# Who subtracts the weights' low parts in the mixer: from GpSimd to VectorE

## The chip, the cores and the metric

One core of a Trainium2 chip runs the whole program. The metric is the device time of one execution in microseconds (us). The kernel before took 1982.04 us, the median of three runs (1978.26 to 1982.62).

## The reference, cut to what matters

Two layers of a hybrid transformer work on 528 tokens (16 meta tokens and 512 others) of width 1024, in float32:

```python
for l in range(DEPTH):                       # DEPTH = 2
    h = mixer_block(h, ...)                  # w_in, three attentions, gates, w_branch, w_o
    h = conv_ffn(h, ...)                     # w_up, conv of width 3, silu(gate) * val, w_down
```

`mixer_block` norms `h`, multiplies it by `w_in` (queries, keys and values of three kinds of attention, and three sets of gates), norms the heads' queries and keys, runs the attentions (8 heads each), multiplies each branch by its `w_branch` and its sigmoid gate, sums them, and multiplies by `w_o`. `conv_ffn` is an up product of 2 x 2816 columns, a causal convolution of width 3, a gated silu, and a down product.

## The kernel before, in words

Activations lie with the width on the 128 partitions and the 528 tokens along the free dimension. All weights are packed on the host into **blocks** of 128x128 in the order in which TensorE takes them, and eight blocks make a **chunk** of 128x1024 float32 (512 KB). A layer has 1080 blocks, 135 chunks: 488 blocks (61 chunks) belong to the mixer's projections, gates and branch products, the rest to `w_o`, the up and the down product. There are 270 chunks in all, numbered c = 0 to 269.

Each product keeps float32 accuracy with three products in the fp32r format: high(x) by high(W), low(x) by high(W), high(x) by low(W) (lines 1357, 1360 and 1362, each as two halves of 264 tokens). So each chunk must be split into a high part `wh`, a copy of `raw` that is rounded to fp32r, and a low part `wl` = `raw` - `wh`. The pipeline for chunk c is:

- SyncE loads it into one of two `raw` buffers (`load`, line 734), once the low part of chunk c - 2 is done, since that was the last reader of the buffer.
- VectorE casts `raw` to `wh` (`high_part`, line 1670). It waits for the load, and for TensorE to have started chunk c - 2, so that one of the three `wh` and `wl` buffers is free.
- GpSimd subtracts (`chunk_low`, line 817) in four pieces of 128x256, since a long instruction of it would hold other work up. Chunk 0 alone has its low part from VectorE (line 1750).
- TensorE waits for the low part at the chunk's first block.

Both splitters work two chunks ahead (`AHEAD = 2`): the place of chunk c in the program of VectorE and of GpSimd is where block 8(c - 2) stands.

The order of everything else in the mixer is one plan (`mixer_plan`): for each event (a norm's statistics, a mask, a row maximum, a reciprocal, a head's copy) it has the block at which it stands, and each engine's program is the sorted list of its own events with the blocks between them. TensorE runs the blocks with the attention's small products in between. VectorE runs the row maxima (line 1962 and, for the meta tokens, 1940), the masks (line 1985), the norms' Newton steps (lines 1686, 1688 and 1691) and the products behind them (1887, 1902, 1906, 1909), the reciprocals of the softmax sums (1993), the scaling of projections (1822, 1830, 1832), and the gated sums (1839, 1844). ScalarE takes exponentials and the high parts of queries, keys and heads. GpSimd subtracts the low parts of these (lines 943, 954, 983, 992, 1001), fills constants into the attention's operands (831, 881 to 886) and copies the decay rows (918). Engines are in order: what stands behind a waiting or a long instruction is late. In the feed-forward part the casts and subtractions stand between the convolution's steps.

Of the kernel before, what the change touches and what calls it, by code (L numbers as in the profile page):

```python
# [9 lines left out]
P = 128  # L10
# [89 lines left out]


LATE = {'sk': 2, 'cq': 2, 'fv': 1}


def constants():
# [69 lines left out]
class Tile:  # L175


    def __init__(self, kind, m, i):
        self.kind, self.m, self.i = kind, m, i
        self.nk = BLOCKS[kind]  # L180
        self.slot = i % 2
        self.freed = None
        self.joint = None
        self.n = None
        self.raw = None


def mixer_plan():
# [105 lines left out]
    for j, (br, p) in enumerate(JOBS):  # L294
        b = BEGIN[j]
        if br == MLA:
            if p < 2:
                put(b - M_LEAD - 9, 4, "ones", j)
        elif j > 0:
            put(b - M_LEAD - 9, 4, "extras", j)  # L300
            put(b - M_LEAD - 5, 4, "extras2", j)
        if br == SWA:
            put(b - M_LEAD - 4, 7, "kfill", j, 0)
            put(b - M_LEAD - 3, 7, "kfill", j, 1)
        parts = [(e, q) for e in range(2) for q in (("4", "3", "2", "1") if br == SWA else ("4a", "4b", "3", "2", "1"))]
# [12 lines left out]
        put(b + PV_LAG, 4, *place(("PVM", j)))  # L318
        i = b + ST_HEAD + 4 + PV_LAG + 2
        for q in range(4):  # L320
            put(i + q, 6, "recip", j, q)
# [4 lines left out]
    blocks = [(i, 9, 0, ("block",) + order[i]) for i in range(len(order))]  # L326

    plan = {"tiles": tiles, "order": order}
    for engine in ("pe", "dve", "act", "pool", "sp"):
        mine = [(i + LAG.get((engine, step[0]), 0), rank, n, step) for i, rank, n, step in events]  # L330
        mine = sorted(blocks + mine, key=lambda x: x[0:3])
        plan[engine] = [x[3] for x in mine]

# [49 lines left out]
    return b  # L383


PLAN = weight_plan(mixer_plan()["order"])
CHUNKS = DEPTH * len(PLAN) // BLK
assert len(PLAN) % BLK == 0


def build(nc, W, H, PRM, CST, POS, OUT, SCR, counts):
# [50 lines left out]
    skh = sb("skh", [P, T], F32R, offset=gsb_at)  # L442
    skl = sb("skl", [P, T], F32R, offset=gsb_at + T * 4)
    mixer_end = at[0]

    at[0] = act_at
    ah = sb("ah", [P, FT, T], F32R)
# [69 lines left out]
    s_hi = nc.alloc_semaphore("chunk_high_part")  # L517
    s_lo = nc.alloc_semaphore("chunk_split")
    s_start = nc.alloc_semaphore("chunk_started")
    ready_made = S("small_tiles_ready")  # L520
    tile_ready = S("tile_ready")
    residual_updated = S("residual_updated")
# [56 lines left out]
    meta_done = S("meta_product_done")  # L579
    meta_heads_copied = S("meta_heads_copied")  # L580
    heads_copied = S("heads_copied")
    heads_ready = S("heads_ready")
    heads_high = S("heads_high_part")
    heads_low = S("heads_low_part")
# [22 lines left out]
    def frees(t):  # L607
        if t.kind == "ff":
            return rope_copied, ()
        if t.kind in NORMED:  # L610
            if t.kind == "cq" and t.m == 0:
                return copied, (t.i,)
            return (stat_copied if t.kind == "mq" else stat_taken), (t.i,)
        if t.kind in ("fv", "sv"):
            return values_scaled, (t.kind, t.m)
        if t.kind == "mv":
            return values_copied, (t.kind, t.m)
        if t.kind == "g":
            return gate_taken, t.m
        return gate_used, t.m  # L620

    previous = {}
    for a, b in zip(tiles, tiles[2:]):
# [100 lines left out]
    with block as blk:  # L724

        @blk.sync
        def _(sp):

            def load(n):
                if n >= CHUNKS:  # L730
                    return
                if n >= RAW:
                    sp.wait_ge(s_lo, n - RAW + 1)
                sp.dma_start(raw[:, n % RAW, :], W[n, :, :]).then_inc(s_raw[n % RAW], 16)

            def advance(l, i):
# [15 lines left out]
            for l in range(DEPTH):  # L752
                n_blocks = 0
                for s in plan["sp"]:
                    if s[0] == "block":
                        advance(l, n_blocks)
                        n_blocks += 1
                    elif s[0] == "extras":
                        j = s[1]
                        br, p = JOBS[j]  # L760
# [39 lines left out]
        def _(pool):  # L800
# [6 lines left out]
                    sem, n = began["last"]  # L807
                    pool.wait_ge(sem, n)

            def chunk_low(c):  # L810
                if c >= CHUNKS:
                    return
                pool.wait_ge(s_hi, c + 1)
                settled()
                for a in range(0, CW, CW // 4):
                    part = slice(a, a + CW // 4)
                    ins = nc.gpsimd.tensor_tensor(wl[c % SPLIT][:, part], raw[:, c % RAW, part],  # L817
                                                  wh[c % SPLIT][:, part].bitcast(F32), ALU.subtract)
                ins.then_inc(s_lo, 1)
                began["last"] = (s_lo, c + 1)  # L820

            def advance(l, i):
                n = l * LB + i
                if n % BLK == 0:
                    chunk_low(n // BLK + AHEAD)

            def fill(t, lo, hi, i, e, c0, c1, value, by=1):

# [21 lines left out]
            settled()  # L850
            pool.sem_inc(zeroed.sem, zeroed.tick((0, 0)))
            for c in range(1, AHEAD):
                chunk_low(c)
            for l in range(DEPTH):
                n_blocks = 0
                for s in plan["pool"]:
# [151 lines left out]
        def _(act):  # L1008
# [29 lines left out]
            act.dma_start(prm[:, :, :], PRM[:, :, :]).then_inc(s_prm, 16)  # L1038
            logarithms()

            def high_input(l, k):

                nc.scalar.activation(xh[:, k, :], h[:, k, :], ACT.Identity,
                                     scale=prm[:, l, PC_N1 + k:PC_N1 + k + 1]).then_inc(
                    high_ready.sem, high_ready.tick((l, "n1", k)))

            act.wait_ge(s_prm, 16)
            for k in range(KD):
                if k % 2 == 0:
# [2 lines left out]
                nc.scalar.activation(merged[:, k, :], h[:, k, :], ACT.Square).then_inc(  # L1052
                    residual_squared.sem, residual_squared.tick((-1, "dn", k)))
            for l in range(DEPTH):
                for s in plan["act"]:
                    if s[0] == "layer stat":
                        if s[1] != (l == 0):
                            continue
                        logarithms()
# [239 lines left out]
                def square_residual(which, k):  # L1299
                    act.wait_ge(residual_updated.sem, residual_updated.at(l, which, k))  # L1300
                    if k >= 2:
                        act.wait_ge(sum_ready.sem, sum_ready.at(l, which, k - 2))
                    nc.scalar.activation(hsq[:, k % 2, :], h[:, k, :], ACT.Square).then_inc(
                        residual_squared.sem, residual_squared.tick((l, which, k)))

                for k in range(KD):
                    act.wait_ge(residual_updated.sem, residual_updated.at(l, "wo", k))
                    nc.scalar.activation(xh[:, k, :], h[:, k, :], ACT.Identity,
                                         scale=gain[:, l, PC_N2 + k:PC_N2 + k + 1]).then_inc(
# [8 lines left out]
                for f in range(FT):  # L1318
                    for side, dst in ((0, cg), (1, cv)):
                        t = 2 * f + side  # L1320
                        m = side * FT + f
                        act.wait_ge(up_scaled.sem, up_scaled.at(l, t))
                        cw = PC_CW + 3 * m
                        nc.scalar.activation(dst[:, f % 2, skip:T], full(SLOTS[t % 4])[:, skip:T], ACT.Identity,  # L1324
# [7 lines left out]
                    copy(ah[:, f, skip:T], cv[:, f % 2, skip:T]).then_inc(act_high.sem, act_high.tick((l, f)))  # L1332
                if l + 1 < DEPTH:
                    act.wait_ge(tile_ready.sem, tile_ready.at(l, "up", 2 * FT - 1))
                    for k in range(KD):
# [6 lines left out]
        def _(pe):  # L1342

            def weights(n):

                c = n // BLK
                if n % BLK == 0:
                    pe.wait_ge(s_lo, c + 1)
                a = n % BLK * P
                return wh[c % SPLIT][:, a:a + P], wl[c % SPLIT][:, a:a + P]  # L1350

# [310 lines left out]
        def _(dve):  # L1662

            def high_part(c):
                if c >= CHUNKS:
                    return
                dve.wait_ge(s_raw[c % RAW], 16 * (c // RAW + 1))
                if c >= SPLIT:
                    dve.wait_ge(s_start, c - SPLIT + 2)
                nc.vector.tensor_copy(wh[c % SPLIT][:, :], raw[:, c % RAW, :]).then_inc(s_hi, 1)  # L1670

            def advance(l, i):
                n = l * LB + i
                if n % BLK == 0 and n > 0:
                    high_part(n // BLK + AHEAD)

            def step(ins, *key):

# [65 lines left out]
            for k in range(KD):  # L1744
                low_input(0, k)
                if k == 0:
                    high_part(0)

                    dve.wait_ge(s_hi, 1)
                    nc.vector.tensor_tensor(wl[0][:, :], raw[:, 0, :], wh[0][:, :].bitcast(F32), ALU.subtract).then_inc(  # L1750
                        s_lo, 1)
                elif k == 3:
                    high_part(1)
                elif k == 6:
# [12 lines left out]
            for l in range(DEPTH):  # L1767
                n_blocks = 0
                for s in plan["dve"]:
# [216 lines left out]
                            scores_masked.sem, scores_masked.tick((l, j, e, t)))  # L1986
                    elif s[0] == "recip":
                        j, q = s[1], s[2]
                        if q == 0:
                            dve.wait_ge(heads_copied.sem, heads_copied.at(l, j, 1))  # L1990
                            dve.wait_ge(meta_heads_copied.sem, meta_heads_copied.at(l, j))
# [2 lines left out]
                            dve_step.sem, dve_step.tick((l, "recip", j, q)))  # L1994
                    elif s[0] == "heads":
                        j = s[1]
                        dve.wait_ge(dve_step.sem, dve_step.at(l, "recip", j, 3))
# [183 lines left out]
```

## Time and profile before

| | before |
|---|---|
| median of 3 runs | 1982.04 us |
| lowest, highest run | 1978.26, 1982.62 us |
| span of the profiled execution | 1979.4 us |
| TensorE busy | 1914.7 us (97%) |
| VectorE busy | 1159.0 us (59%) |
| GpSimd busy | 1025.5 us (52%) |
| ScalarE busy | 766.2 us (39%) |

The profiled execution gives a span, from its first instruction to its last, and the runs a device time. The median of the runs is 2.6 us above this span. A matmul's end is modelled, so a busy TensorE may hide short waits: what counts are its waits and the chain of waits, which the profile follows back from the last instruction.

In the trace each layer's mixer takes some 520 us (0 to about 525, and about 1008 to about 1510), and the feed-forward part with `w_o` the rest (to about 1008 and to the end).

### The profile page before, as it was taken

What the parts mean: (1) busy time and instruction counts of PE and PEld (TensorE: products, weight loads), DVE (VectorE), ACT (ScalarE), POOL (GpSimd) and SP (SyncE); (2) the same over time, 40 slices, a digit from 0 to 9 for tenths busy, and PEclk for the clock granted to TensorE, in tenths of its full rate; (3) what the DMA queues carried; (4) which work ended last, traced back from release to release, by engine and by line L of the source; (5) the groups of instructions that cost most, each with busy time, mean ns of one, the idle gap of its engine ahead of it and who ended that gap; (6) DMA issues with size and microseconds to landing.
All of it is one profiled execution on the core that took longest, in us unless ns stands there. A gap on an engine that the chain in (4) does not pass through costs nothing.

```text
span 1979.4 us, 36478 instructions
## 1 busy us (share of the span) xinstructions
PE 1914.7 (97%) x14396; PEld 1817.1 (92%) x14396; DVE 1159.0 (59%) x2121; ACT 766.2 (39%) x1514; POOL 1025.5 (52%) x1306
## 2 busy tenths in 40 slices
PE   7899999999999999999998999999999999999999
PEld 7889998888999999999997899988889999999887
DVE  7665476787465666552256654767874655665411
ACT  5455666655223222220044556666553232222100
POOL 7655454544364444544477455544443645445553
PEclk9999999999999999999999999999999999999999
DMA  4212121211232322332332121112112423323332
GB/s 149 75 44 65 54 65 44 63 45 55 65 129 85 97 86 86 97 93 93 93 109 76 43 65 54 63 46 65 45 53 65 141 86 97 97 86 96 96 97 96
DMA packets 44802, 156.30 MB, mean 79 GB/s; under 512 B 5012, under 2 KB 5268, under 8 KB 44504
## 3 DMA queue, kind: packets, MB, share of 16 engines
q1 hardware_dynamic: 44488, 153.75, 24.7%
q8 instruction: 114, 1.87, 0.4%
q14 instruction: 56, 0.46, 0.1%
q10 hardware_dynamic: 144, 0.22, 0.0%
HBM read 149.63 MB, written 4.26 MB: 78 GB/s over the span
## 4 chain that ended last, share of the span: by engine, by line
PE 77%; DVE 12%; ACT 4%; issue 3%; POOL 2%; DMA 1%; SPq 0%; DVEq 0%; ACTq 0%; POOLq 0%
PE ps L1357 20%; PE ps L1360 19%; PE ps L1362 19%; PE ps L1588 5%; PE ps L1372 2%; PE ps L1368 2%; PE ps L1371 2%; PE ps L1376 2%; DVE osum L1993 1%; DVE rstd L1691 1%; PE ps L1540 1%; PE ps L1501 1%; POOL wl L817 1%; DVE ps L1962 1%; DVE square L1686 1%
## 5 line engine op out<-in xcount | busy, mean ns | idle before, releaser
L817 POOL TENSOR_TENSOR wl<-raw,wh 128x256 fp32r<-128x256 f32 x1076 | 798.7, 773 | 746.5 <-DVE wh L1670 739.9
L1357 PE MATMUL ps<-xh,wh 128*128 128x264 f32 (+1 forms) x2880 | 810.7, 303 | 12.5 <-DVE wl L1750 9.4
L1360 PE MATMUL ps<-xl,wh 128*128 128x264 f32 (+1 forms) x2880 | 764.3, 286 | 0.0
L1362 PE MATMUL ps<-xh,wl 128*128 128x264 f32 (+1 forms) x2880 | 585.4, 285 | 0.0
L1357 PEld LDWEIGHTS ps<-xh,wh 128*128 128x128 f32 x2880 | 546.7, 190 | 31.1 <-issue 18.3
L1360 PEld LDWEIGHTS ps<-xl,wh 128*128 128x128 f32 x2880 | 547.4, 190 | 17.0 <-issue 8.9
L1362 PEld LDWEIGHTS ps<-xh,wl 128*128 128x128 f32 x2880 | 451.2, 190 | 0.0
L1670 DVE CAST wh<-raw 128x1024 fp32r<-128x1024 f32 x270 | 206.6, 765 | 176.0 <-PE ps L1357 89.1
L1588 PE MATMUL ps<-pt,vx 128*128 128x512 f32 (+7 forms) x480 | 157.8, 409 | 3.9 <-ACT pt L1274 2.3
L1985 DVE TENSOR_TENSOR ps<-ps,cst 128x128 f32<-128x128 f32 (+6 forms) x240 | 74.8, 313 | 145.3 <-PE ps L1546 111.0
L1274 ACT ACTIVATE pt<-ps 128x256 f32<-128x256 f32 (+5 forms) x224 | 78.5, 363 | 112.5 <-DVE ps L1985 111.2
L1324 ACT ACTIVATE cv<-ps,prm 128x528 f32<-128x528 f32 (+1 forms) x44 | 34.6, 786 | 209.0 <-DVE ps L2039 209.0
L1357 PE MATMUL ps<-oth,wh 128*128 128x264 f32 (+1 forms) x384 | 111.5, 312 | 2.1 <-ACT ssum L1011 1.7
L2039 DVE TENSOR_TENSOR ps<-ps,rstd 128x528 f32<-128x528 f32 (+1 forms) x88 | 62.1, 706 | 80.5 <-PE ps L1362 80.4
L1360 PE MATMUL ps<-otl,wh 128*128 128x264 f32 (+1 forms) x384 | 100.9, 283 | 0.0
L1993 DVE RECIPROCAL osum<-osum 128x132 f32<-128x132 f32 x96 | 90.0, 958 | 13.2 <-ACT oraw L1011 13.0
L1360 PE MATMUL ps<-al,wh 128*128 128x264 f32 x352 | 93.1, 285 | 0.0
L1357 PE MATMUL ps<-ah,wh 128*128 128x264 f32 x352 | 93.0, 284 | 0.0
L1540 PE MATMUL ps<-xq,xk 97*17 97x16 f32 (+15 forms) x288 | 78.2, 290 | 8.8 <-ACT ptm L1255 4.0
L1501 PE MATMUL ps<-xk,xq 96*128 96x400 f32 (+13 forms) x256 | 71.6, 300 | 9.1 <-DVE nm L1962 3.0
L1588 PEld LDWEIGHTS ps<-pt,vx 128*128 128x128 f32 x480 | 74.6, 191 | 6.2 <-ACT pt L1274 4.1
L1001 POOL TENSOR_TENSOR otl<-oraw,oth 128x528 fp32r<-128x528 f32 x24 | 34.5, 1437 | 87.5 <-ACT oth L1011 86.7
(194 smaller groups left out, 3440.9 us busy)
## 6 DMA issues: line engine op xcount, KB each, us to landing
raw<-weights SPq DMA_DIRECT2D x270, 512.0 KB, 3.5
h<-tokens SPq DMA_DIRECT2D x4, 528.0 KB, 6.9
h<-tokens SPq DMA_DIRECT2D x8, 264.0 KB, 6.0
residual<-h SPq DMA_DIRECT2D x8, 264.0 KB, 5.0
h<-residual SPq DMA_DIRECT2D x8, 264.0 KB, 5.9
out<-h SPq DMA_DIRECT2D x8, 256.0 KB, 4.7
cst<-constants SPq DMA_DIRECT2D x1, 1048.0 KB
extra<-positions SPq DMA_DIRECT2D x18, 4.1 KB
```

The lines of the kernel that those rows point to most:

```text
L817: ins = nc.gpsimd.tensor_tensor(wl[c % SPLIT][:, part], raw[:, c % RAW, part], wh[c % SPLIT][:, part].bitcast(F32), ALU.subtract)
L1274: ins = nc.scalar.activation(pt[0:nk, i, 0:nq], bank[0:nk, 0:nq], ACT.Exp)
L1357: a = nc.tensor.matmul(out, a_hi, x_hi[:, sl], start=first, stop=False)
L1360: nc.tensor.matmul(out, a_hi, x_lo[:, sl], start=False, stop=False)
L1362: ins = nc.tensor.matmul(out, a_lo, x_hi[:, sl], start=False, stop=last)
L1501: ins = nc.tensor.matmul(bank[:, col:col + nk], xq[rows, i, e, q], xk[rows, i, e, k0:k0 + nk], start=True, stop=True)
L1540: nc.tensor.matmul(out, xk[rows, i, e, keys], xq[rows, i, e, q], start=True, stop=False)
L1588: ins = nc.tensor.matmul(heads_out[:, c:c + nq], vals, pt[:, i, 0:nq], start=t == 0, stop=t == 4)
L1670: nc.vector.tensor_copy(wh[c % SPLIT][:, :], raw[:, c % RAW, :]).then_inc(s_hi, 1)
L1985: nc.vector.tensor_tensor(sc, sc, cst[0:nk, a:a + n], ALU.add).then_inc(scores_masked.sem, scores_masked.tick((l, j, e, t)))
L1993: nc.vector.reciprocal(osum[:, a:a + T // 4], osum[:, a:a + T // 4]).then_inc(dve_step.sem, dve_step.tick((l, "recip", j, q)))
L2039: nc.vector.tensor_tensor(src[:, skip:T], src[:, skip:T], rstd[:, skip:T], ALU.mult).then_inc(up_scaled.sem, up_scaled.tick((l, t)))
```

## The change

In the mixer, VectorE makes the low part as well, in one subtraction of 128x1024 directly behind the cast of the same chunk, and GpSimd doesn't touch these chunks. Chunks 0 to 2 and all chunks outside the mixer are split as before. The rest of the diff generalizes: each chunk's high and low part has an engine by a table, each engine has a semaphore of its own for them, and waits go to the semaphore of the engine that does the part. A second feature (`fold`, which packs the softmax sums before their reciprocals) is in the code but off, since `UNFOLDED` lists all twelve jobs; so are the empty table `NUDGE` and the high parts on ScalarE and GpSimd.

```diff
+UNFOLDED = list(range(12))
...
+HIGH_AT = {"dve": 0, "act": 0, "pool": 0}
+LOW_AT = {"dve": 0, "pool": 0}
+POOL_PIECE = 256
+FIRST = 3
+MIX_HIGH, FFN_HIGH = "dve", "dve"
+MIX_DVE, FFN_DVE = 1024, 0
...
+def low_by(c):
+
+    d = CW if c == 0 else 0 if c < FIRST else MIX_DVE if in_mixer(c) else FFN_DVE
+    return {"dve": (0, d), "pool": (d, CW)}
...
                 if n >= RAW:
-                    sp.wait_ge(s_lo, n - RAW + 1)
+                    for sem, value in low_done(n - RAW):
+                        sp.wait_ge(sem, value)
...
-            def chunk_low(c):
+            def low_part(c):
                 if c >= CHUNKS:
                     return
-                pool.wait_ge(s_hi, c + 1)
+                first, end = low_by(c)["pool"]
+                if end <= first:
+                    return
+                pool.wait_ge(*high_done(c))
                 settled()
...
+            def low_part(c):
                 if c >= CHUNKS:
                     return
-                dve.wait_ge(s_raw[c % RAW], 16 * (c // RAW + 1))
-                if c >= SPLIT:
-                    dve.wait_ge(s_start, c - SPLIT + 2)
-                nc.vector.tensor_copy(wh[c % SPLIT][:, :], raw[:, c % RAW, :]).then_inc(s_hi, 1)
+                a, b = low_by(c)["dve"]
+                if b <= a:
+                    return
+                dve.wait_ge(*high_done(c))
+                nc.vector.tensor_tensor(wl[c % SPLIT][:, a:b], raw[:, c % RAW, a:b], wh[c % SPLIT][:, a:b].bitcast(F32),
+                                        ALU.subtract).then_inc(chunk_low["dve"].sem, chunk_low["dve"].tick((c,)))
 
             def advance(l, i):
                 n = l * LB + i
-                if n % BLK == 0 and n > 0:
+                if n % BLK == HIGH_AT["dve"] and n >= BLK:
                     high_part(n // BLK + AHEAD)
+                if n % BLK == LOW_AT["dve"]:
+                    low_part(n // BLK + AHEAD)
```

Two places show what moves. The first is VectorE in the first layer's mixer, at the second MLA job, where TensorE waits for the row maximum `nm` and the scaled tile `rawt`. Before:

```order
L1993 RECIPROCAL osum<-osum 128x132 x2
L1670 CAST wh_54<-raw 128x1024
L1830 TENSOR_TENSOR rawt<-ps,gq 32x528
L1832 TENSOR_TENSOR rawt<-ps,gq 96x528
L1962 ISA ps,nm_99<-ps,cst 128x144
```

and with the change:

```order
L2156 RECIPROCAL osum<-osum 128x132 x2
L1818 CAST wh_54<-raw 128x1024
L1828 TENSOR_TENSOR wl_57<-raw,wh_54 128x1024
L1988 TENSOR_TENSOR rawt<-ps,gq 32x528
L1990 TENSOR_TENSOR rawt<-ps,gq 96x528
L2120 ISA ps,nm_99<-ps,cst 128x144
```

One instruction more stands between the cast and what TensorE waits for. There are 119 such pairs (the 2 x 61 chunks of the mixers less the first three); nothing else on VectorE changes its place.

The second place is GpSimd at the start of the second layer's mixer (`xk`, `xq` and `yk`, `yq` are the attention's operands and their low parts, `extra` the decay rows). Before:

```order
L954 TENSOR_TENSOR yk<-q_87,xk 64x528 x2
L831 CAST xk<-unit 1x530
L817 TENSOR_TENSOR wl_55<-raw,wh_52 128x256 x4
L918 CAST xk<-extra 2x528 x2
L831 CAST xk<-unit 1x530
L943 TENSOR_TENSOR yq<-q_87,xq 64x528 x2
L831 CAST xq<-unit 2x528 x2
L817 TENSOR_TENSOR wl_56<-raw,wh_53 128x256 x4
L817 TENSOR_TENSOR wl_57<-raw,wh_54 128x256 x4
L943 TENSOR_TENSOR yq<-q_87,xq 64x528 x2
```

and with the change:

```order
L1072 TENSOR_TENSOR yk<-q_87,xk 64x528 x2
L949 CAST xk<-unit 1x530
L1036 CAST xk<-extra 2x528 x2
L949 CAST xk<-unit 1x530
L1061 TENSOR_TENSOR yq<-q_87,xq 64x528 x2
L949 CAST xq<-unit 2x528 x2
L1061 TENSOR_TENSOR yq<-q_87,xq 64x528 x2
```

The weights' subtractions are gone from between GpSimd's other work, which keeps its order.

## Rows read from the trace of the kernel before

**Rows 1.** The page: busy time, share of the span, instructions of each engine.

```profile
PE 1914.7 (97%) x14396; PEld 1817.1 (92%) x14396; DVE 1159.0 (59%) x2121; ACT 766.2 (39%) x1514; POOL 1025.5 (52%) x1306
```

**Rows 2.** Busy time by stretch: stretch and its length, then engines, granted clock, DMA.

```profile
50.00:525.00 475.00, 453.54 (x3304) 419.07 (x3305) 316.62 (x692) 263.69 (x580) 246.54 (x285) 0.99 0.19 58
600.00:990.00 390.00, 390.00 (x3191) 389.82 (x3191) 192.80 (x275) 79.49 (x116) 188.73 (x267) 1.00 0.30 91
1075.00:1510.00 435.00, 416.97 (x3085) 385.30 (x3083) 291.54 (x640) 246.82 (x542) 219.45 (x256) 1.00 0.18 57
```

**Rows 3.** TensorE's waits between 50 and 525 us: total, times, longest.

```profile
PE ps L1376 <- DVE rawt L1832: 4.1, 4, 1.1
PE ps L1509 <- DVE nm L1940: 2.3, 2, 2.1
...
PE ps L1469 <- DVE nm L1962: 1.5, 1, 1.5
```

**Rows 4.** The splitting's groups of instructions, whole span: busy, mean, idle before.

```profile
L817 POOL TENSOR_TENSOR wl<-raw,wh 128x256 fp32r<-128x256 f32 x1076 | 798.7, 773 | 746.5 <-DVE wh L1670 739.9
L1670 DVE CAST wh<-raw 128x1024 fp32r<-128x1024 f32 x270 | 206.6, 765 | 176.0 <-PE ps L1357 89.1
```

**Rows 5.** Start of the program, VectorE in order: start, us, instruction.

```profile
8.03 1.23 DVE L1750 TENSOR_TENSOR wl<-raw,wh 128x1024 fp32r<-128x1024 f32 x1
```

**Rows 6.** The chain of waits at the first and last counted cast, and the dense stretch.

```profile
54.67 0.70 DVE wh L1670
...
413.38 0.92 DVE osum L1993
414.30 0.55 DVE wh L1670
414.84 0.03 issue
414.88 0.71 DVE rawt L1830
...
416.53 0.07 DVE nm L1962
...
1472.15 0.69 DVE wh L1670
```

**Rows 7.** VectorE at 407 us, and GpSimd then, in order of time.

```profile
407.44 1.23 DVE L1688 SCALAR_TENSOR_TENSOR square<-ssum,square 128x528 f32<-128x528 f32 x1
408.71 0.71 DVE L1691 SCALAR_TENSOR_TENSOR rstd<-square,rstd 128x528 f32<-128x528 f32 x1
405.31 2.79 POOL L817 TENSOR_TENSOR wl<-raw,wh 128x256 fp32r<-128x256 f32 x4 [0.63 <-DVE wh L1670]
```

**Rows 8.** Line 1691 over the span: min, median, max of one in ns.

```profile
L1691 DVE SCALAR_TENSOR_TENSOR rstd<-square,rstd x56: 707/709/1733, 35.0 to 1611.1; 128x528 f32<-128x528 f32 x56
```

**Rows 9.** The chain of waits at the start of the second mixer.

```profile
1008.16 2.83 POOL wl L817 x4
...
1054.58 3.93 POOL wl L817 x4
1058.53 3.46 DMA raw<-weights
1062.01 0.04 DVE wh L1670
```

**Rows 10.** The same two waits of TensorE in the first and second mixer.

```profile
50.49 0.39 PE L1357 MATMUL ps<-xh,wh 128*128 128x264 f32 x1 [1.19 <-DVE merged L1822]
111.22 0.33 PE L1509 MATMUL ps<-cst,nm 128*128 128x128 f32 x1 [2.08 <-DVE nm L1940]
1038.27 0.39 PE L1357 MATMUL ps<-xh,wh 128*128 128x264 f32 x1 [1.13 <-DVE merged L1822]
1102.60 0.47 PE L1509 MATMUL ps<-cst,nm 128*128 128x128 f32 x1 [2.06 <-DVE nm L1940]
```

More of the change, by code:

```diff
@@ L102, with folded @@
 LATE = {'sk': 2, 'cq': 2, 'fv': 1}
+NUDGE = {}
+FOLD = [3, 7, 13]
+FOLD_N = 2 * T // (P - MQ)
+UNFOLDED = list(range(12))
+def folded(j):
+    return j not in UNFOLDED
 def constants():
@@ L185, in __init__, with step_name @@
         self.raw = None
+def step_name(step):
+    words = [step[0]]
+    for x in step[1:]:
+        if isinstance(x, Tile):
+            words.append(f"{x.kind}{x.m[0]}{x.m[1]}" if isinstance(x.m, tuple) else f"{x.kind}{x.m}")
+        elif not isinstance(x, dict):
+            words.append(str(x))
+    return " ".join(words)
 def mixer_plan():
@@ L319, in mixer_plan @@
         i = b + ST_HEAD + 4 + PV_LAG + 2
-        for q in range(4):
-            put(i + q, 6, "recip", j, q)
+        if folded(j):
+            put(i, 2, "fold", j)
+            put(i + FOLD[0], 6, "recip", j, 0)
+            put(i + FOLD[0], 7, "unfold", j)
+            put(i + FOLD[1], 8, "spread", j)
+            i += FOLD[2] - 4
+        else:
+            for q in range(4):
+                put(i + q, 6, "recip", j, q)
         if j >= OT_RING:
@@ L444, in build, with fold @@
     mixer_end = at[0]
+    fold_at = MQ
+    inverse = nc.dram_tensor("inverse", (DEPTH, len(JOBS), 2, T), F32, kind="Internal").ap()
+    def fold(j):
+        return krr[fold_at:P, j % 2 * FOLD_N:(j % 2 + 1) * FOLD_N]
     at[0] = act_at
@@ L620, in frees, with chunk_raw, high_done, low_done @@
         return gate_used, t.m
+    def chunk_raw(c):
+        return s_raw[c % RAW], 16 * (c // RAW + 1)
+    def high_done(c):
+        s = chunk_high[high_by(c)]
+        return s.sem, s.at(c)
+    def low_done(c):
+        return [(chunk_low[e].sem, chunk_low[e].at(c)) for e, (a, b) in low_by(c).items() if b > a]
     previous = {}
@@ L808, in settled, with high_part @@
                     pool.wait_ge(sem, n)
-            def chunk_low(c):
+            def high_part(c):
+                if c >= CHUNKS or high_by(c) != "pool":
+                    return
+                pool.wait_ge(*chunk_raw(c))
+                if c >= SPLIT:
+                    pool.wait_ge(s_start, c - SPLIT + 2)
+                settled()
+                nc.gpsimd.tensor_copy(wh[c % SPLIT][:, :], raw[:, c % RAW, :]).then_inc(
+                    chunk_high["pool"].sem, chunk_high["pool"].tick((c,)))
+                began["last"] = (chunk_high["pool"].sem, chunk_high["pool"].n)
+            def low_part(c):
                 if c >= CHUNKS:
                     return
-                pool.wait_ge(s_hi, c + 1)
+                first, end = low_by(c)["pool"]
+                if end <= first:
+                    return
+                pool.wait_ge(*high_done(c))
                 settled()
-                for a in range(0, CW, CW // 4):
-                    part = slice(a, a + CW // 4)
+                for a in range(first, end, POOL_PIECE):
+                    part = slice(a, min(end, a + POOL_PIECE))
                     ins = nc.gpsimd.tensor_tensor(wl[c % SPLIT][:, part], raw[:, c % RAW, part],
                                                   wh[c % SPLIT][:, part].bitcast(F32), ALU.subtract)
-                ins.then_inc(s_lo, 1)
-                began["last"] = (s_lo, c + 1)
+                ins.then_inc(chunk_low["pool"].sem, chunk_low["pool"].tick((c,)))
+                began["last"] = (chunk_low["pool"].sem, chunk_low["pool"].n)
             def advance(l, i):
                 n = l * LB + i
-                if n % BLK == 0:
-                    chunk_low(n // BLK + AHEAD)
+                if n % BLK == HIGH_AT["pool"] and n >= BLK:
+                    high_part(n // BLK + AHEAD)
+                if n % BLK == LOW_AT["pool"]:
+                    low_part(n // BLK + AHEAD)
             def fill(t, lo, hi, i, e, c0, c1, value, by=1):
@@ L852, in _ @@
             for c in range(1, AHEAD):
-                chunk_low(c)
+                low_part(c)
             for l in range(DEPTH):
@@ L1039, in _, with high_part, advance @@
             logarithms()
+            def high_part(c):
+                if c >= CHUNKS or high_by(c) != "act":
+                    return
+                act.wait_ge(*chunk_raw(c))
+                if c >= SPLIT:
+                    act.wait_ge(s_start, c - SPLIT + 2)
+                copy(wh[c % SPLIT][:, :], raw[:, c % RAW, :]).then_inc(
+                    chunk_high["act"].sem, chunk_high["act"].tick((c,)))
+            def advance(l, i):
+                n = l * LB + i
+                if n % BLK == HIGH_AT["act"] and n >= BLK:
+                    high_part(n // BLK + AHEAD)
             def high_input(l, k):
@@ L1304, in square_residual, with advance_by @@
                         residual_squared.sem, residual_squared.tick((l, which, k)))
+                count = {"n": n_blocks}
+                def advance_by(n):
+                    for _ in range(n):
+                        advance(l, count["n"])
+                        count["n"] += 1
                 for k in range(KD):
+                    advance_by(2 * KD if k == 0 else KD if k > 1 else 0)
                     act.wait_ge(residual_updated.sem, residual_updated.at(l, "wo", k))
@@ L1334, in _ @@
                     act.wait_ge(tile_ready.sem, tile_ready.at(l, "up", 2 * FT - 1))
-                    for k in range(KD):
+                for k in range(KD):
+                    advance_by(FT)
+                    if l + 1 < DEPTH:
                         act.wait_ge(residual_updated.sem, residual_updated.at(l, "dn", k))
@@ L1347, in weights @@
                 if n % BLK == 0:
-                    pe.wait_ge(s_lo, c + 1)
+                    for sem, value in low_done(c):
+                        pe.wait_ge(sem, value)
                 a = n % BLK * P
@@ L1988, in _ @@
                         j, q = s[1], s[2]
+                        if folded(j):
+                            dve.wait_ge(sums_folded.sem, sums_folded.at(l, j))
+                            nc.vector.reciprocal(fold(j), fold(j)).then_inc(
+                                dve_step.sem, dve_step.tick((l, "recip", j, 0)))
+                            continue
                         if q == 0:
```

66 lines of the change are left out of this document (57 added, 9 removed).

## The prediction

> **What bounds the kernel now.** I read the busy shares first, then the stretches, then TensorE's waits, then the chain of waits. TensorE is busy 97% of the span [rows 1], so nearly all of it is TensorE's own work and only its waits can move. The stretches say where they are: in the feed-forward part, between 600 and 990 us, TensorE has no idle time at all, in the two mixers it idles 21.5 of 475 and 18.0 of 435 us [rows 2]. The reader is to see there that a cheaper or dearer GpSimd cannot matter between 600 and 990 as long as chunks are in time, and that the whole question lies in the mixers. What TensorE waits for there is mostly VectorE: a scaled tile, a row maximum, each 1 to 2 us at a time [rows 3]. It never waits there for GpSimd, nor for a weight's low part. The chain of waits agrees: where it leaves TensorE in the mixers it runs through VectorE, often through several instructions in a row, with casts among them [rows 6]. There, VectorE has no slack at all, though over the stretch it is only two thirds busy (316.6 of 475, 291.5 of 435) [rows 2]. So the mean says that there is room for the subtractions and the chain says that there is none at the places that count.
>
> **What is added.** 119 subtractions of 128x1024 on VectorE. The trace has exactly one of them, chunk 0's, 1.23 us [rows 5]; with the hand-over from the cast I take 1.24 us. In total that is 148 us on VectorE. GpSimd loses 119 x 4 pieces of 0.773 us, 368 us [rows 4]. With them VectorE is about four fifths busy in the two stretches: 51 casts stand in the first, 316.6 + 51 x 1.24 = 380 of 475 us.
>
> **What of it lies on the path.** I counted the casts that the chain of waits passes through from 50 us on in the first mixer and from 1060 us in the second: 11 in each, the first at 54.67 and the last at 1472.15 us [rows 6]. In each the chain goes on with the next instruction of VectorE, and now the subtraction stands between the two. The clearest is at 414 us: reciprocal, cast, `rawt`, then `nm`, for which TensorE has been waiting 1.5 us [rows 3, 6]. Cost: 22 x 1.24 = **+27.3 us**. The other 97 start where VectorE has some idle time behind them. For 43 of them it is less than 1.24 us within the next 4 us, so that they leave VectorE late for a while. This is the cost that the trace does not show. Its low bound is 0 (each delay dies in VectorE's idle time before TensorE asks), its high bound 43 x 1.24 = 53 us. I take **+8 us**, near the low bound, since at those places the rows show no wait of TensorE yet.
>
> **What is taken away.** First, contention. A VectorE instruction with two SBUF operands that runs beside GpSimd's subtraction is stretched: line 1688 took 1.23 us beside the pieces of `wl`, and line 1691 directly behind it, when they had ended, 0.71 us [rows 7]; the least and the median of line 1691 are 0.71 us, its longest 1.73 [rows 8]. On the chain in the two mixers 26 instructions of VectorE overlap a piece of `wl` and are longer than the same instruction alone, by 0.1 to 0.5 us, 9.3 us together: **-9.3 us**. GpSimd's own subtractions for queries, keys and heads stay, and so does the stretching by them, now and then over a new subtraction too; I book nothing for it. The Trainium skill, page "SBUF — State Buffer", section "Who interferes with whom", says that VectorE and GpSimd share one port pair, and that of a VectorE cast or two-input instruction and a GpSimd instruction that reads SBUF the one that starts second is fully blocked until the first ends. By that rule each overlap costs up to the rest of one piece of 0.77 us. Rows 7 agree in kind: 0.52 us for that overlap. With the full 0.77 us for each of the 26, the sum would be 11 us lower.
>
> Second, the start of the second mixer. There the chain runs for 50 us through GpSimd, six chunks' low parts among fills and copies, and at its end a load that waited for a low part reaches VectorE's cast late, at 1062.01 us [rows 9]. With the low parts gone GpSimd is early and the load can start behind VectorE's subtraction. What that gives is not the 21 us of `wl` on the chain, since the next chain stands close behind. I bound it by the first mixer, where the same work has no GpSimd on the chain: from one wait of TensorE to the other it took 60.73 us (50.49 to 111.22), in the second 64.33 (1038.27 to 1102.60) [rows 10]. **-3.6 us**, and the low bound is 0.
>
> Edits at nothing: SyncE's and TensorE's waits keep their number and only change the semaphore; a load in the mixer waits for a low part that now ends 0.77 + 1.24 = 2.0 us behind the cast's start instead of 0.77 + 3.09 = 3.9 us, so it is earlier. The feed-forward part keeps its instructions, and TensorE's full 390 us cover them [rows 2].
>
> **The sum.** 1979.4 + 27.3 + 8 - 9.3 - 3.6 = 2001.8 us for the profiled span; the median of the runs stood 2.6 us above the span, so **2004 us**, 1.1% slower than the 1982.0 before. A measurement of this kernel can tell about 0.2%, 4 us, from no change.
>
> **Rivals.**
>
> *The subtractions are hidden, and GpSimd's absence counts (faster).* For it: VectorE idles 158 and 143 us in the two stretches [rows 2], and an instruction that is late by 1.2 us may be made up by the stretching that is gone from it, 23 us over all VectorE instructions of the mixers. If the chain's 22 casts were passed without loss, what stays is -9.3 - 3.6 = -12.9, so 1969 us. The point from which it decides is whether a cast on the chain has 1.24 us of slack; at 414 us the next instructions follow within 0.03 us [rows 6], which speaks against it. The Trainium skill says in "GPSIMD Engine Reference", section "Key points", that VectorE is about twice as fast at elementwise work. By that rule, the trace agrees on the duration. Chance 0.18: a chunk's subtraction does cost 1.23 us on VectorE against 3.09 us on GpSimd [rows 4, 5], but GpSimd's time is hidden and VectorE's on the chain is not.
>
> *Gains and losses cancel (no difference).* If half of the 22 are absorbed, +13.6, against -12.9: 1983 us. Chance 0.08.
>
> *VectorE becomes the bound in the dense parts (much slower).* At four fifths busy, delays no longer die between two chunks: a chunk comes every 475 / 51 = 9.3 us, and where VectorE has no idle time the delays of several chunks add up. Then the 43 subtractions that leave it late cost all of their 1.24 us: 2004 - 8 + 53 = 2049 us; with half of them 2023 us. Against it: most events of VectorE depend on TensorE's own progress, so it must idle again. Chance 0.2 that it comes to 2023 us or more.
>
> *The change does nothing*: the programs of the engines show the 119 subtractions moved, so this has no share.
>
> **How the numbers follow.** Forecast 0.54 (1987 to 2023), hidden 0.18, cancel 0.08, dense 0.2. The range from 1975 to 2038 leaves out the lower half of the hidden case and the upper part of the dense one. Faster by over 0.2% 0.18, within 0.2% 0.08, slower 0.74.
>
> **What would show it.** In the profile after: VectorE busy up by about 148 less some 20 us, near 1285 us, GpSimd down by 368 to about 655. Subtractions on the chain in the mixers, some 22 or more of them; TensorE's waits for `rawt` and `nm` longer by about one subtraction each; TensorE's idle time in 50 to 525 us up from 21 to over 30 us. Line 1691's counterpart nearer to 0.71 us. No GpSimd on the chain at the second mixer's start. The feed-forward stretch unchanged. The forecast is wrong if TensorE's waits for VectorE in the mixers do not grow, or if the mixers' stretches are shorter.

## The result, and the profile after

The changed kernel took 2053.48 us (median of four runs, 2048.18 to 2054.30) against 1981.61 us before: 1.036 times as long, 95% interval 1.035 to 1.038 (the kernel before has a fourth run here, so its median is not quite the 1982.04 us told above). The direction was forecast, the size was not: 2004 us was said, with a range up to 2038.

The profiled execution spans 2051.9 us, 72.5 more than before. The page of the changed kernel, to be held against [rows 1] and [rows 4]. Lines have moved: 1670 is now 1818, 817 is 933, 1750 is 1828, 1832 is 1990, 1962 is 2120, 1940 is 2098, and in the runs below they stand up to four further on. The first line is the kernel before's chain of waits, by engine; the others are the changed kernel's:

```profile
PE 77%; DVE 12%; ACT 4%; issue 3%; POOL 2%; DMA 1%; SPq 0%; DVEq 0%; ACTq 0%; POOLq 0%
...
PE 1938.8 (94%) x14396; PEld 1831.4 (89%) x14396; DVE 1284.6 (63%) x2240; ACT 766.7 (37%) x1514; POOL 687.9 (34%) x830
PE 70%; DVE 19%; issue 6%; ACT 4%; DMA 0%; SPq 0%; DVEq 0%; ACTq 0%
L933 POOL TENSOR_TENSOR wl<-raw,wh 128x256 fp32r<-128x256 f32 x600 | 433.9, 754 | 453.7 <-DVE wh L1818 453.1
L1828 DVE TENSOR_TENSOR wl<-raw,wh 128x1024 fp32r<-128x1024 f32 x120 | 164.5, 1370 | 4.1
```

VectorE's busy time came out as forecast (about 1285 us was said). GpSimd's is 688 us where 655 was said. VectorE's 63% looks harmless. But the chain of waits says otherwise: VectorE now carries 19% of it, where it had 12%. I count 68 of the 119 new subtractions on it. The last two rows are groups of instructions: a new subtraction took 1.370 us on average, not 1.23.

Busy time by stretch, where the two mixers are cut at the same work as in [rows 2], and the feed-forward stretch between them:

```profile
50.00:561.00 511.00, 464.33 (x3307) 424.72 (x3308) 371.55 (x743) 263.72 (x580) 105.46 (x83) 0.98 0.17 54
636.00:1026.00 390.00, 390.00 (x3191) 389.83 (x3190) 193.19 (x276) 79.52 (x116) 189.24 (x268) 1.00 0.29 91
1110.00:1582.00 472.00, 430.99 (x3083) 393.68 (x3082) 338.60 (x684) 247.37 (x544) 91.03 (x71) 0.97 0.17 52
```

The numbers are the length, then the busy time (and instructions) of TensorE, its weight loads, VectorE, ScalarE and GpSimd, then the granted clock, the DMA share and GB/s. In the feed-forward stretch TensorE runs the same 3191 matmuls in the same 390 us: no loss there. The mixers are 36 and 37 us longer. TensorE idles 46.7 and 41.0 us in them (21.5 and 18.0 before), and its granted clock is lower. TensorE's waits in the first mixer, as in [rows 3]:

```profile
PE ps L1524 <- DVE rawt L1990: 7.7, 5, 3.3
PE ps L1657 <- DVE nm L2098: 5.6, 5, 1.8
PE ps L1649 <- DVE nmx L2120: 3.5, 6, 1.9
```

The 72.5 us split exactly in two. TensorE's idle time over the span, span less busy time, rose from 64.7 to 113.1 us: 48.4 us. Its busy time for the same 14396 matmuls rose from 1914.7 to 1938.8 us: 24.1 us. Longer busy time for the same work points to the granted clock, whose mean fell (before, then after):

```profile
core 0: 1979.4 us, clock 0.995
core 0: 2051.9 us, clock 0.986
```

That is 0.014 x 2051.9 = 28.7 us of clock not granted against 0.005 x 1979.4 = 9.9: an estimate of 18.8 us out of the 24.1. It is rather a high one: two executions of the changed kernel at 0.989 and 0.984 took 2048.18 and 2054.30 us, 6.1 us apart, where this sum gives 10. What the other 5 us and more are stays open.

The example that shows it best is a place that I had marked as on the chain. The first line is TensorE in the kernel before; it waited 0.98 us for `rawt`. The others are the changed kernel: VectorE in order of time, then GpSimd and TensorE (start, us, instruction):

```profile
335.62 1.13 PE L1376 MATMUL ps<-sq,cst 96*128 96x264 f32 x4 [0.98 <-DVE rawt L1832]
...
349.66 0.68 DVE L1818 CAST wh<-raw 128x1024 fp32r<-128x1024 f32 x1
350.37 2.28 DVE L1828 TENSOR_TENSOR wl<-raw,wh 128x1024 fp32r<-128x1024 f32 x1
352.69 0.71 DVE L1988 TENSOR_TENSOR rawt<-ps,gq 32x528 f32<-32x528 f32 x1
353.41 0.70 DVE L1990 TENSOR_TENSOR rawt<-ps,gq 96x528 f32<-96x528 f32 x1
350.25 1.32 POOL L1101 TENSOR_TENSOR yq<-q,xq 96x528 fp32r<-96x528 f32 x1 [12.72 <-ACT xq L1129]
354.26 1.14 PE L1524 MATMUL ps<-sq,cst 96*128 96x264 f32 x3 [3.30 <-DVE rawt L1990]
```

The wait has grown by 2.32 us, the whole subtraction with its hand-over. And that subtraction took 2.28 us instead of 1.23. It began 0.12 us behind one of GpSimd's own: GpSimd ended at 351.57, VectorE 1.08 us later. The page "SBUF — State Buffer" of the Trainium skill, section "Who interferes with whom", says that the one that starts second is fully blocked until the first ends; this trace agrees nearly: a full block until 351.57 would have cost 1.20 us, and 1.05 us were lost. Over all 120 subtractions 120 x (1.370 - 1.226) = 17 us of VectorE's time went that way (1.226 is their median). GpSimd pays too: its busy time of 687.9 us is 28.6 more than with the same instructions in the run below where nobody makes the mixers' low parts (659.3).

### The profile page after: what moved, and what is told of

The parts are those of the page before. It is cut to its first block, busy times and chain, and to the rows that moved or that the text cites. A ratio compares the mean times of both kernels' runs of the same rounds, so it can differ in the third digit from the quotient of the medians.

```text
span 2051.9 us, 36002 instructions
## 1 busy us (share of the span) xinstructions
PE 1938.8 (94%) x14396; PEld 1831.4 (89%) x14396; DVE 1284.6 (63%) x2240; ACT 766.7 (37%) x1514; POOL 687.9 (34%) x830
## 4 chain that ended last, share of the span: by engine, by line
PE 70%; DVE 19%; issue 6%; ACT 4%; DMA 0%; SPq 0%; DVEq 0%; ACTq 0%
PE ps L1505 18%; PE ps L1508 18%; PE ps L1510 18%; PE ps L1736 5%; DVE wh L1818 3%; DVE wl L1828 2%; DVE osum L2156 2%; PE ps L1520 2%; PE ps L1516 2%; PE ps L1519 2%; PE ps L1524 2%; DVE ps L2120 2%; DVE rstd L1852 1%; PE ps L1649 1%; PE ps L1688 1%
## 5 line engine op out<-in xcount | busy, mean ns | idle before, releaser
L933 POOL TENSOR_TENSOR wl<-raw,wh 128x256 fp32r<-128x256 f32 x600 | 433.9, 754 | 453.7 <-DVE wh L1818 453.1
L1828 DVE TENSOR_TENSOR wl<-raw,wh 128x1024 fp32r<-128x1024 f32 x120 | 164.5, 1370 | 4.1
L1061 POOL TENSOR_TENSOR yq<-q,xq 64x528 fp32r<-64x528 f32 x32 | 49.9, 1558 | 146.7 <-ACT xq L1129 143.6
```

Source lines behind the costliest of these rows:

```text
L1828: nc.vector.tensor_tensor(wl[c % SPLIT][:, a:b], raw[:, c % RAW, a:b], wh[c % SPLIT][:, a:b].bitcast(F32), ALU.subtract).then_inc(chunk_lo ...
```

## Experiments

All kernels are the changed one with the edit shown. Times are medians; "before" is the kernel before on the same chip, between 1981.3 and 1982.8 us.

Theory A: what counts is which instructions that TensorE waits for stand behind a new subtraction in VectorE's program. Rivals: B, the rewrite of the waits and semaphores costs; C, VectorE's long subtraction and GpSimd's remaining ones stretch each other; D, each subtraction costs the same wherever it stands.

**The rewrite alone.**

```diff
-MIX_DVE, FFN_DVE = 1024, 0
+MIX_DVE, FFN_DVE = 0, 0
```

> The changed program with GpSimd making the mixers' low parts again: one table entry (MIX_DVE) is 0, everything else of the rewrite stays. Theory A (the 119 subtractions delay, in VectorE's program, what TensorE waits for): back to 1982 us within 4 us. Rival B (the rewrite itself costs: other semaphores, other waits of SyncE and TensorE): stays well above 1990 us, up to 2053. Rival C (VectorE's long subtraction and GpSimd's own remaining ones stretch each other): also 1982, since the long subtraction is gone.

Measured: 1981.35 us, ratio 1.0002 (0.9992 to 1.0011). B has fallen: the loss is all in the 119 subtractions. C isn't touched by this run, since it forecast the same.

**Nobody makes the mixers' low parts.**

```diff
+    if c >= FIRST and in_mixer(c):
+        return {"dve": (0, 0), "pool": (CW, CW)}
...
+        if c >= FIRST and in_mixer(c):
+            return [high_done(c)]
```

> Nobody makes the low part of the mixers' chunks (119 subtractions left out on both engines, TensorE waits for the high part instead and reads what the buffers hold). This prices what taking GpSimd's subtractions away is worth, alone. My terms were -9.3 us (stretched instructions on the chain) and -3.6 us (start of the second mixer): 1969 us. Theory A says that and that the whole loss of the change, 2053 - 1969 = 84 us, is the price of VectorE's subtractions. Rival B: not below 1982. Rival C: 1969 too, since neither long subtraction is there.

Measured: 1964.09 us, 0.9919 (0.9905 to 0.9934) of before. The relief is real, 17.3 us, somewhat more than my 12.9. So the subtractions on VectorE cost 2053.5 - 1964.1 = 89 us, 0.75 us each on average, with whatever they and GpSimd's other work do to each other.

**Both make them.**

```diff
+    if c >= FIRST and in_mixer(c):
+        return {"dve": (0, CW), "pool": (0, CW)}
...
                 pool.wait_ge(*high_done(c))
+                if c >= FIRST and in_mixer(c):
+                    pool.wait_ge(chunk_low["dve"].sem, chunk_low["dve"].at(c))
```

> VectorE makes the low part as in the change, and GpSimd makes it once more in its four pieces, as before, after VectorE's semaphore; TensorE waits for both. Cost without relief. Theory A: the change's 2053 us plus what the relief was worth, about 13 us, so some 2066 us. If the relief is worth nothing: 2053. Rival C: more than that, up to 2090, since GpSimd's work beside VectorE's two-operand instructions is then five times as much as in the change.

Measured: 2085.02 us, 1.054 (1.052 to 1.057), 31.5 us above the change where the relief alone is 17: theory A's 2066 us is missed, and the result lies in C's range. GpSimd's pieces cost about twice what they cost in the kernel before. VectorE's busy time is 1324.3 us, 39.7 more than in the change, and the new subtraction itself is only 4 us of that:

```profile
L1832 DVE TENSOR_TENSOR wl<-raw,wh 128x1024 fp32r<-128x1024 f32 x120 | 168.5, 1404 | 4.1
```

so most of it is other instructions of VectorE that GpSimd's four pieces stretch. But the run doesn't isolate C. The pieces now end later, TensorE waits for them, and the chain of waits has GpSimd on it again:

```profile
PE 65%; DVE 20%; issue 6%; ACT 5%; POOL 3%; DMA 1%; SPq 0%; DVEq 0%; ACTq 0%; POOLq 0%
```

How the 31.5 us split between the two was not measured.

**Half of the columns.**

```diff
-MIX_DVE, FFN_DVE = 1024, 0
+MIX_DVE, FFN_DVE = 512, 0
```

> VectorE makes the first 512 of the 1024 columns of the mixers' low parts, GpSimd the other two pieces. A VectorE subtraction of 512 columns should take about 0.7 us (528 columns took 0.71). Theory A with a price in proportion: 1982 + 72 x 0.7 / 1.24 = 2023 us. Theory A with a threshold (delays die in VectorE's idle time while they are short): under 2010 us. Rival C: about half of its part is gone, no clear number, 2005 to 2025.

Measured: 2009.19 us, 1.0142 (1.0120 to 1.0163): +28 us, not the +41 of proportion. That lies at the edge of what a threshold was to give (under 2010 us). In the profiled execution TensorE idles 86.3 us against 64.7:

```profile
span 2000.3 us, 36517 instructions
PE 1914.0 (96%) x14396; PEld 1813.3 (91%) x14396; DVE 1231.7 (62%) x2240; ACT 766.6 (38%) x1514; POOL 892.3 (45%) x1068
```

So TensorE's idle time grew by 21.6 us for half the columns and 48.4 for all, about in proportion. This execution, though, is the fastest of four, at a mean clock of 0.997. The other three took 2007.7 to 2011.8 us at 0.990 to 0.994. Beside 13 executions of the kernel before on the same chip (0.995 to 0.998) the clock fell with half the columns too, by less than in the change (0.984 to 0.989). How the 28 us split between idle time and clock this run doesn't settle.

**Three groups of chunks.** These are the test of my sum. The 119 chunks were split by the trace of the kernel before: 22 whose casts were on the chain, 46 that were not but had less than 1.24 us of VectorE's idle time in the next 4 us (43 in my text; this count is over all chunks), and 51 with more.

```diff
-    d = CW if c == 0 else 0 if c < FIRST else MIX_DVE if in_mixer(c) else FFN_DVE
+    d = CW if c == 0 else 0 if c < FIRST else MIX_DVE if c in CHOSEN else FFN_DVE
```

> VectorE makes the low parts of the 22 chunks alone whose casts lay on the chain of waits of the kernel before; GpSimd makes all others. It tests the first term of my sum by itself. My count: 22 x 1.24 = +27 us, less a fifth of the relief (3 us): 2006 us. Rival D (the price is the same for each of the 119, (2053 - 1982) / 119 = 0.6 us, wherever it stands): 1982 + 13 = 1995 us.

> VectorE makes the low parts of the 46 chunks whose casts were not on the chain but had less than 1.24 us of VectorE's idle time within the next 4 us. My sum had +8 us for them, less relief of 6: 1984 us. If I underrated them, and they carry what the forecast missed: 2005 us and more (46 x 0.6 = 28 by rival D gives 2010; 46 x 1.24 = 57 less relief gives 2033).

> VectorE makes the low parts of the 51 chunks with 1.24 us and more of VectorE's idle time within the 4 us after the cast; GpSimd makes the others. Theory A (a delay that dies in idle time costs nothing): 1982 less 51/119 of the relief of 17 us = 1975 us, faster than the kernel before. Rival D: 1982 + 51 x 0.6 = 2013 us. Between them, about 1990, if half of that idle time was waiting whose end moves with the delay.

Measured, against 1982.38 us before:

| chunks | us | ratio (95%) | difference | each |
|---|---|---|---|---|
| 22 on the chain | 2012.07 | 1.0154 (1.0139 to 1.0169) | +29.7 | 1.35 |
| 46 late | 1998.91 | 1.0086 (1.0071 to 1.0101) | +16.5 | 0.36 |
| 51 with idle time | 2003.17 | 1.0105 (1.0088 to 1.0122) | +20.8 | 0.41 |
| all 119 | 2053.48 | 1.0362 (1.0347 to 1.0378) | +71.9 | 0.60 |

The three sum to 67.0 of 71.9 us: the cost is nearly additive. D has fallen, since a subtraction on the chain costs over three times one elsewhere. The first term stands. The third group was to be free, and isn't.

Why, the trace of that run shows at chunk 45. VectorE in the kernel before, and below it TensorE's use of `nm`:

```profile
425.06 0.69 DVE L1670 CAST wh<-raw 128x1024 fp32r<-128x1024 f32 x1
425.66 0.30 DVE L1962 CUSTOM_DVE_ANT_0 ps<-ps,cst 128x144 f32<-128x144 f32 x1
425.88 0.14 DVE L1962 DVE_READ_ACCUMULATOR2_ANT nm<- 128x1 f32 x1
...
426.08 0.21 DVE L1940 DVE_READ_ACCUMULATOR2_ANT nm<- 16x1 f32 x1
...
429.53 0.71 DVE L1791 TENSOR_TENSOR ssum<-ps,extra 128x528 f32<-128x528 f32 x1 [2.70 <-PE ps L1376]
426.54 0.27 PE L1509 MATMUL ps<-cst,nm 128*128 128x128 f32 x1
```

and in the run with the 51:

```profile
431.39 0.68 DVE L1819 CAST wh<-raw 128x1024 fp32r<-128x1024 f32 x1
432.11 2.25 DVE L1829 TENSOR_TENSOR wl<-raw,wh 128x1024 fp32r<-128x1024 f32 x1
434.29 0.30 DVE L2121 CUSTOM_DVE_ANT_0 ps<-ps,cst 128x144 f32<-128x144 f32 x1
...
434.71 0.21 DVE L2099 DVE_READ_ACCUMULATOR2_ANT nm<- 16x1 f32 x1
434.97 0.47 PE L1658 MATMUL ps<-cst,nm 128*128 128x128 f32 x1 [1.93 <-DVE nm L2099]
```

I had counted the 2.70 us of idle time that come at 426.8. But the row maxima `nm` stand between the cast and that idle time. The last of them, the meta tokens', was done at 426.29 us, and TensorE took them at 426.54, 0.25 us later and without a wait. Idle time that comes later helps nothing that stands before it. In the run with the 51 the last maximum is done 2.3 us later behind its cast than before, and TensorE waited 1.93 us. Then the granted clock fell. Stretches of 2 us of the same run (the granted clock is the third number from the end):

```profile
432.00:434.00 2.00, 1.04 (x9) 0.83 (x7) 1.97 (x2) 0.92 (x2) 1.28 (x1) 1.00 0.00 0
434.00:436.00 2.00, 1.03 (x5) 0.93 (x6) 1.46 (x8) 0.29 (x2) 0.00 (x0) 0.75 0.30 51
436.00:438.00 2.00, 2.00 (x11) 2.00 (x11) 0.00 (x0) 1.54 (x6) 0.00 (x0) 0.50 0.55 211
438.00:440.00 2.00, 2.00 (x14) 1.87 (x13) 0.53 (x1) 0.00 (x0) 0.00 (x0) 0.89 0.00 0
```

0.5 is 1.2 GHz of 2.4: TensorE started 11 matmuls between 436 and 438 us, 1.0 us behind its first use of `nm`. In the kernel before, 1.0 us behind the same place, it started 15 in 2 us, at the full clock.

**The subtraction four blocks behind the cast.**

```diff
-LOW_AT = {"dve": 0, "pool": 0}
+LOW_AT = {"dve": 4, "pool": 0}
```

> The change, but VectorE's subtraction stands four blocks (some 4 us) behind its cast instead of directly behind it (LOW_AT of VectorE is 4), for chunk 2 and up. Theory A: no block of 2.0 us any more that holds up a short instruction, but the same sum of work in the dense stretches and other neighbours: some 10 us off, 2040 us, if bursts matter; 2053 if only the sum does. Rival D: 2053.

Measured: 2025.43 us, 1.0220 (1.0205 to 1.0235). The same work on the same engine, 28 us less. TensorE's idle time fell from 113.1 to 86.2 us (span 2021.7, busy 1935.5); the clock stayed at 0.986. So 28 of the 72 us hang on the place alone. A part of that is C's: the subtractions take 1.298 us on average here, not 1.370, 8.6 us less in total, since fewer meet one of GpSimd's.

**The 51 chunks, four blocks behind.** Both edits together.

> The 51 chunks with idle time behind the cast (2003 us with the subtraction directly behind it), now with the subtraction four blocks behind. Theory A in its present form: idle time later does not help an instruction that stands right behind the subtraction, such as the row maximum nm behind chunk 45; four blocks on, the subtraction falls nearer to or into that idle time, so well under 2003 us, 1985 to 1995. If placement does not matter: 2003 us.

Measured: 1987.61 us, 1.0045 (1.0025 to 1.0064). From +20.8 to +6.3 us by the medians (+8.9 by the ratio) by placement alone. Of its ten executions eight took 1984 to 1992 us at a mean clock of 0.994 to 0.998, and two took 2001 us at 0.987: the same program, 14 us longer with the lower clock.

**The ends of the mixers.** `CHOSEN` is 52 to 60 and 135 to 143.

> VectorE makes the low parts of 18 chunks only: the last nine of the first mixer (52 to 60) and the first nine of the second (135 to 143). In the change's trace its casts do not fall further behind those of the kernel before over either stretch. With GpSimd freed at the second mixer's start, my second relief term is alone here: it was -3.6 us; in the run without low parts the casts gained 5 us between chunks 137 and 144. Theory A: 1981.5 - 4 = 1977.5 us. If the term was GpSimd's share elsewhere: no difference. Rival D (0.6 us for each subtraction): 1992 us.

Measured: 1976.91 us over twelve runs, 0.9984 (0.9975 to 0.9993), 4.4 us faster than before by the medians, 3.2 (1.4 to 5.0) by the ratio. It beats both kernels. GpSimd has left the chain at the second mixer's start, as forecast: in [rows 9] there were six chunks of `wl` on it, now the chain's shares there are

```profile
by line: issue 15.9%; DVE wh L1819 8.9%; DVE wl L1829 6.9%; DVE ssum L1956 4.9%; ACT square L1149 4.7%; ACT square L1147 4.7%; ACT rstd L1148 4.7%; PE ps L1506 4.0%; DVE square L1848 3.9%; DVE rstd L1853 3.9%; PE ps L1525 3.7%; PE ps L1511 
```

with no line of GpSimd among the largest. The profiled execution places the gain: VectorE's casts, held against the kernel before, move ahead by 1.4 us between chunks 134 and 146. Larger jumps elsewhere, of some 3 us, stand where one of the two traces has a stretch at half the clock and the other has not.

**Ends and picked chunks.** `CHOSEN` has also 4 to 6, 9, 10, 12 to 16, 144, 145, 147, 148, 150 and 151.

> As the run before it, and also chunks 4 to 6, 9, 10, 12 to 16, 144, 145, 147, 148, 150 and 151, over which the casts of the two runs of single groups gained or lost nothing against the kernel before. Theory A, if such gains add up: 1974 us. If the neighbourhoods interact (a chunk that is free alone is late behind another one's subtraction): 1978 to 1985 us. Rival D: 2001 us.

Measured: 1982.95 us, 1.0008 (1.0000 to 1.0017). The forecast for gains that add up (1974 us) is missed, the one for chunks that disturb each other (1978 to 1985) holds. Which chunks it is stays open.

**Two chunks only.** `CHOSEN` is 45 and 180.

> VectorE makes the low parts of two chunks only, 45 and 180, the same place in the two mixers; in the run of the 51 chunks its casts fell back by 3.6 and 3.8 us behind these two. Theory A, with its second part (TensorE's wait for the row maximum behind the subtraction brings a stretch at half the granted clock with it): up to 7.4 us for two subtractions, 1988.5 us. If only the subtraction itself counts: 2 x 1.24 = 2.5 us, 1984 us. If these two were late only because of the others before them: 1981 us.

Measured: 1988.55 us against 1982.79, 1.0032 (1.0019 to 1.0045). 6.3 us (3.8 to 8.9) by the ratio, for two subtractions. The place looks as it did with the 51:

```profile
421.72 2.24 DVE L1829 TENSOR_TENSOR wl<-raw,wh 128x1024 fp32r<-128x1024 f32 x1
421.53 1.34 POOL L1102 TENSOR_TENSOR yq<-q,xq 96x528 fp32r<-96x528 f32 x1 [2.62 <-ACT xq L1130]
424.56 0.48 PE L1658 MATMUL ps<-cst,nm 128*128 128x128 f32 x1 [1.92 <-DVE nm L2099]
426.00:428.00 2.00, 2.00 (x11) 2.00 (x11) 0.00 (x0) 1.15 (x5) 0.00 (x0) 0.51 0.44 180
```

(VectorE, GpSimd, TensorE, and the stretch behind). At chunk 180 TensorE waits 2.11 us and the half clock follows too. VectorE's casts fall back against the kernel before by 3.6 us behind the first place and 3.9 behind the second. So such a subtraction costs 3 us and more: 1.24 of its own and 1.0 blocked by GpSimd, of which TensorE waits 1.9 to 2.1, and the rest fits the half clock that follows. In the kernel before the same stretches have the full clock. The bound of 1984 us for the subtraction alone has fallen.

## Why the prediction was right and wrong

**Right: the direction, and what bounds the kernel.** The waits for `rawt` and `nm` grew, the mixers got longer, the feed-forward part did not, and GpSimd left the chain at the second mixer's start.

**Right in kind, a little small: the 22 on the chain.** +27.3 us was said. Measured are +29.7 us, which hold 22/119 of the relief, 3.2 us, so about 33: 1.5 us each. For the missing part there are two things that I booked at nothing: GpSimd's own subtractions block the new ones (1.346 us on average in that run, 1.226 alone), and the clock (0.992 in its profile). How it divides between them was not measured.

**The step that failed: the other 97.** "The other 97 start where VectorE has some idle time behind them" was taken as cover, with +8 us for 43 and nothing for the rest. Measured are +16.5 and +20.8 us, and with their shares of the relief (6.7 and 7.4 us) they cost some 23 and 28 us. So the larger error is in the group that I put at nothing because it had idle time behind it. The error has two parts. Idle time within 4 us was counted without asking what stands between the subtraction and it: chunk 45. And I took as a reason for the low end that TensorE showed no wait at the late places. No wait says nothing of how large the slack is: at chunk 45, where there was none either, TensorE took `nm` 0.25 us after the last of it was made.

In sum: the forecast had +22.4 us for the change, 71.9 were measured. Of the 49.5 between them the 22 on the chain have 5.6, the 46 late ones 15, the 51 with idle time 28, and 4.9 is what the three runs together leave over; the larger relief takes 4.4 off.

**The term that was missing: the clock.** Up to 18.8 us of the 72, and it lies within the three groups' costs, not beside them. The prediction spoke of waits only, and the kernel before already had stretches below the full clock. The rival "dense parts", at 2049 us and with a chance of 0.2, was near the measured time, but its mechanism, delays that add up from chunk to chunk, is not what the runs show: three separate groups sum to nearly the whole.

**Right in kind, small: the relief.** -12.9 said, -17.3 us measured by the run without low parts. For the start of the second mixer -3.6 was said, and the run with the ends alone gave 4.4 by the medians, 3.2 by the ratio. The sign of line 1691 didn't come: its counterpart still takes 0.71 us in the median and 1.74 at its longest, as before.

**Open.** How much of the loss is blocking between VectorE and GpSimd was not isolated by a run of its own, such as one without GpSimd's subtractions for queries and keys. The 17 us of stretched subtractions are a sum over the trace, and only 68 of the subtractions were on the chain. So rival C has a part in the loss, and its size is not shown.

## What to carry to other kernels

An engine's busy share, or its idle time nearby, is no cover for a new instruction. For each place look at the next instructions behind it up to the first idle time, and at how long after each the waiting engine takes its result: that gap is the slack. Slow work on an idle engine can be the better bargain: here GpSimd's 3.1 us a chunk cost 17 us in total, VectorE's 1.2 us cost 89; moving only 18 chunks, at the ends where the trace showed no loss, made the kernel 3 to 4 us faster, while moving all 119 made it 72 us slower.

## What the runs showed of the hardware that I had not expected

Some waits of TensorE of about 2 us, in the middle of dense work, were followed by 3 to 10 us at half the clock (0.50 at 436 us behind a wait of 1.93 us), and others of the same length were not. One place shows both. In the kernel before, TensorE waited 1.97 us until 299.95 us; in the run with two chunks, whose first new subtraction comes at 421 us, it waited 1.96 us until 298.80. The stretches of 2 us that begin 2 us behind these waits, before and then in that run:

```profile
302.00:304.00 2.00, 2.00 (x6) 1.03 (x5) 0.00 (x0) 0.37 (x3) 1.87 (x4) 0.50 0.00 0
300.80:302.80 2.00, 2.00 (x16) 1.91 (x15) 0.32 (x1) 0.50 (x3) 1.87 (x4) 1.00 0.00 0
```

VectorE's casts behind this place come 3.0 us earlier in the run that kept its clock. So the time of the same work moves with whether a wait brings the half clock with it, and a trace of one execution can show it or not. Longer waits brought it more reliably here: in the changed kernel's trace, behind 50 us, all six waits of 2.5 us and more were followed by half clock within 5 us, and three of the sixteen between 1.5 and 2.5 us. That makes a longer wait dearer than its length, by the clock that may follow; how much dearer was not measured.
